# Second attention spread behind weight tiles, first attention with two pairs of score banks, in a kernel of two transformer blocks

## The reference, cut to what matters

```python
s = q @ k.T * scale (+ bias)
p = softmax(s)                  # differential: p1 - lam * p2, then an RMS norm of the output
o = p @ v
x = x + gt_a * (concat(o) @ w_out)
```

```python
q_a, k_a, v_a, q_b, k_b, v_b, f_logit, g_a, g_b = split(hn @ w_in)
a = causal_attention(q_a, k_a, v_a, bias=-slope * distance)     # 8 "moba" heads
b = causal_attention(q_b, k_b, v_b, bias=c_q - c_k)             # 8 "fox" heads, c = cumsum(log_sigmoid(f_logit))
merged = sigmoid(g_a) * (a @ w_proj_a) + sigmoid(g_b) * (b @ w_proj_b)
x = x + merged @ w_out
```

## Time and profile before

| | before |
|---|---|
| median of 3 runs | 2947.49 us |
| the profiled execution's own time | 2962.96 us |
| its span in the profile | 2961.1 us |
| TensorE, matmuls busy | 2801.1 us (95%) |
| VectorE busy | 1785.9 us (60%) |
| ScalarE busy | 1155.6 us (39%) |
| mean granted TensorE clock | 0.977 of full |
| first attention | from 479.6 to 639.6 us, with three of its four output units |
| second attention | from 1780.3 us, its own steps alone until the first gate unit at 1853.7 us |

### The profile page before, as it was taken

How to read it: one execution, slowest core, us unless ns; L and a number is a source line. 1 busy time by engine, 2 the same in 40 slices (tenths; PEclk the granted TensorE clock), 3 DMA queues, 4 the chain that set the end, 5 groups by cost and what they waited for, 6 DMA issues and landing times.

```text
span 2961.1 us, 33601 instructions
## 1 busy us (share of the span) xinstructions
PE 2801.1 (95%) x12559; PEld 2248.7 (76%) x12559; DVE 1785.9 (60%) x1973; ACT 1155.6 (39%) x1485; POOL 393.8 (13%) x298
## 2 busy tenths in 40 slices
PE   5999999898999999999989998999999999999997
PEld 1587786577777888888767886888787888888885
DVE  2479964766699555555564447455455566566565
ACT  3132233434333444444343434444443444444443
POOL 2124304101777000000060000000000000000000
PEclk9999998999999999999999999999999999999998
DMA  9988962235776655555445560555555655556552
GB/s 353 313 289 302 320 227 86 71 143 196 260 240 225 216 195 184 191 192 194 159 171 180 189 198 29 185 194 190 169 181 180 194 184 188 195 184 188 194 184 99
DMA packets 286271, 579.88 MB, mean 196 GB/s; under 512 B 14034, under 2 KB 18546, under 8 KB 283886
## 3 DMA queue, kind: packets, MB, share of 16 engines
q1 hardware_dynamic: 277176, 542.55, 55.3%
q0 software_dynamic: 7152, 35.33, 3.3%
q10 hardware_dynamic: 1862, 0.92, 0.1%
HBM read 573.63 MB, written 5.14 MB: 195 GB/s over the span
## 4 chain that ended last, share of the span: by engine, by line
issue 59%; PE 25%; POOLq 6%; DVE 4%; DMA 3%; POOL 2%; ACT 1%; DVEq 1%; SPq 0%; ACTq 0%
PE bank L361 6%; PE bank L363 6%; PE bank L362 6%; POOLq L2074 2%; PE bank L619 2%; POOLq L2076 2%; DMA w_raw<-in_w_ada 1%; POOLq L2083 1%; DVE proj_ctx L1449 1%; POOLq L2081 1%; DMA b_rows<-in_b_ada 1%; PE bank L1755 1%; PE bank L655 1%; ACT probs L729 1%; DVE w_lo L357 1%
## 5 line engine op out<-in xcount | busy, mean ns | idle before, releaser
L357 DVE TENSOR_TENSOR w_lo<-w_raw,w_hi 128x1024 fp32r<-128x1024 f32 (+2 forms) x856 | 1139.5, 1354 | 636.4 <-ACT w_hi L349 624.4
L349 ACT ACTIVATE w_hi<-w_raw 128x1024 fp32r<-128x1024 f32 (+2 forms) x856 | 894.3, 1056 | 1313.1 <-PE bank L363 1150.5
L361 PE MATMUL bank<-w_hi,xa_hi 128*128 128x512 f32 (+1 forms) x2304 | 907.4, 394 | 27.4 <-DVE w_lo L357 22.8
L363 PE MATMUL bank<-w_hi,xa_lo 128*128 128x512 f32 (+1 forms) x2304 | 898.3, 390 | 0.0
L362 PE MATMUL bank<-w_lo,xa_hi 128*128 128x512 f32 (+1 forms) x2304 | 898.3, 390 | 0.0
L361 PEld LDWEIGHTS bank<-w_hi,xa_hi 128*128 128x128 f32 x2304 | 435.2, 189 | 131.2 <-DVE w_lo L357 19.7
L363 PEld LDWEIGHTS bank<-w_hi,xa_lo 128*128 128x128 f32 x2304 | 435.0, 189 | 90.4
L362 PEld LDWEIGHTS bank<-w_lo,xa_hi 128*128 128x128 f32 x2304 | 435.4, 189 | 88.1 <-issue 0.7
L361 PE MATMUL bank<-w_hi,ffn_act_hi 128*128 128x512 f32 x864 | 339.5, 393 | 12.9 <-DVE w_lo L357 12.9
L362 PE MATMUL bank<-w_lo,ffn_act_hi 128*128 128x512 f32 x864 | 338.1, 391 | 0.0
L363 PE MATMUL bank<-w_hi,ffn_act_lo 128*128 128x512 f32 x864 | 337.9, 391 | 0.0
(11 more groups left out here) (274 smaller groups left out, 1896.7 us busy)
## 6 DMA issues: line engine op xcount, KB each, us to landing
w_raw<-in_w_in SPq DMA_DIRECT2D x116, 1024.0 KB, 5.1
w_raw<-in_w_ada SPq DMA_DIRECT2D x80, 1024.0 KB, 6.6
w_raw<-in_w_up SPq DMA_DIRECT2D x64, 1024.0 KB, 5.3
w_raw<-in_w_down SPq DMA_DIRECT2D x64, 1024.0 KB, 5.2
w_raw<-in_ffn_wg SPq DMA_DIRECT2D x44, 1024.0 KB, 5.2
w_raw<-in_ffn_wu SPq DMA_DIRECT2D x44, 1024.0 KB, 5.2
w_raw<-in_ffn_wd SPq DMA_DIRECT2D x44, 1024.0 KB, 5.1
w_raw<-in_w_out SPq DMA_DIRECT2D x32, 1024.0 KB, 5.1
```

Of the source, the lines that this page charges most:

```text
L349: act.activation(whi[:, slot, ks, 0:w], raw[:, q, ks, 0:w], ACT.Copy)\
L357: dve.tensor_tensor(wlo[:, slot, ks, 0:w], raw[:, q, ks, 0:w], whi[:, slot, ks, 0:w].bitcast(F32), ALU.subtract).then_inc(sem("lo_made"), 1)
L361: pe.matmul(out, xh, wh, start=first, stop=False)
L363: return pe.matmul(out, xl, wh, start=False, stop=last)
```

## The change

The class `Attn` and its three functions go; each attention gets its own functions of one step.

**Second attention.** Units of the column blocks 6 to 11 and of the first gate block (28 units, v = 0 to 27) are written out, and behind 19 of them stands one step of the attention: behind v = 1, 3, ... 15 the steps n = 0 to 7, behind v = 17 to 27 the steps n = 8 to 18. Scores use one bank, turned probabilities one, turned keys and queries one, outputs one. The cumulated forget sum of all fox heads is made once (n = 1) and added by one float32 matmul for each half of the scores.

**First attention.** Scores get two pairs of banks, turned probabilities a single bank used twice in a step (first copied out by ScalarE, then by VectorE), outputs one bank. Probabilities are turned at n-3, values made at n-4. Step 0's keys and queries are turned ahead of the last unit, (9, 3). `hi` and `lo` of the first two output units move into steps 3 and 5.

```diff
+HOOK_BEHIND = {2 * n + 1: n for n in range(8)} | {9 + n: n for n in range(8, N_HEADS2 + 3)}
+        OUT_SPLIT = {3: 0, 5: 1, len(STEPS) + 1: 2, len(STEPS) + 2: 3}
+        def s_bank(n, i):
+            return ps[2 + 2 * (n % 2) + i]
+        def att1_pe(pe, n):
+            s = valued(n - 6)
+            if s and s["kind"] == "diff":
+                pe.wait_ge(sem("diff_normed"), s["head"] + 1)
...
+            if s and s["turn"]:
+                wait(pe, "att_qk_copied", s["a"])
...
+            s = valued(n - 3)
+            if s:
+                pe.wait_ge(sem("att_probs"), n - 2)
+                wait(pe, "att_pt_copied_d", s["d"])
+                att1_turn_probs(pe, n - 3, 0)
+            s = step(n - 1)
+            if s:
+                pe.wait_ge(sem("att_qk_copied"), s["a"] + 1)
+                wait(pe, "att_exp_done", n - 2)
...
+            s = valued(n - 3)
+            if s:
+                pe.wait_ge(sem("att_pt_copied_a"), s["d"] + 1)
+                att1_turn_probs(pe, n - 3, 1)
+            s = valued(n - 4)
...
+        def att1_act(act, n):
...
+        def att1_dve(dve, n):
...
+        def att2_pe(pe, n):
+            if 0 <= n - 1 < N_HEADS2:
+                s, r = STEPS2[n - 1], (n - 1) % 2
+                pe.wait_ge(sem("att2_qk_copied"), n)
+                wait(pe, "att2_negmax", n - 1)
...
+                for i in range(2):
+                    bank = ps[5][:, i * SEQ:(i + 1) * SEQ]
+                    m = pe.matmul(bank, qT2[:, r, i * P:i * P + P], kT2[:, r, :], start=True, stop=not fox)
+                    if fox:
+                        m = pe.matmul(bank, ident[:, s["head"]:s["head"] + 1].to_broadcast([P, P]), decay[:, :],
+                                      start=False, stop=True)
+            if n < N_HEADS2:
+                wait(pe, "att2_qk_copied", n)
...
+            d = n - 2
+            if 0 <= d < N_HEADS2:
+                pe.wait_ge(sem("att2_probs"), d + 1)
+                wait(pe, "att2_pt_copied", d)
...
+            if n == 1:
+                for j in range(2):
+                    m = pe.matmul(ps[7][0:8, 0:SEQ], nlf[:, j, :], tri[:, j, :], start=j == 0, stop=j == 1)
+            d = n - 3
+            if 0 <= d < N_HEADS2:
+                pe.wait_ge(sem("att2_pt_copied"), d + 1)
+                wait(pe, "att2_out_lo", d)
...
@@ ScalarE
-            hi(act, U_OUT // 4, 0)
             behind(len(W) - 2)
-            hi(act, U_OUT // 4, 1)
+            act.wait_ge(sem("rotated_pe"), 1)
+            att1_act(act, 0)
             behind(len(W) - 1)
...
+            for n in range(1, H1 + 6):
+                att1_act(act, n)
+                if n in OUT_SPLIT:
+                    hi(act, U_OUT // 4, OUT_SPLIT[n])
...
+            for v in range(29):
+                u = U_WIN2 + 24 + v
+                hi(act, u // 4, u % 4)
+                if v % 4 == 1 and v < 28:
+                    c = 5 + v // 4
+                    qkv2_copy(c, c % 2)
+                if v - 1 in HOOK_BEHIND:
+                    att2_act(act, HOOK_BEHIND[v - 1])
@@ VectorE: the same with lo, att1_dve and att2_dve
@@ TensorE
+                if (c, k) == (9, 2):
+                    pe.wait_ge(sem("mla_copied_a"), 3)
+                    pe.wait_ge(sem("mla_copied_d"), 3)
+                    pe.wait_ge(sem("rotated_pe"), 1)
+                    att1_pe(pe, 0)
+            for n in range(1, H1 + 6):
+                att1_pe(pe, n)
+                if n - H1 in (0, 1, 2):
...
+                    unit(pe, U_OUT // 4, q, ps[0:2], XA, 4 * BY_HEADS[q], q == 0, False)
...
+            for v in range(28):
...
+                unit(pe, U_WIN2 // 4 + c, q, ps[2 * b:2 * b + 2], XA, 4 * q, q == 0, q == 3)
+                if v in HOOK_BEHIND:
+                    att2_pe(pe, HOOK_BEHIND[v])
@@ GpSimd
+            pool.wait_ge(sem("x2_stored"), 16)
+            pool.memset(decay[:, :], 0.0)
```

More of the change, by code:

```diff
@@ L827, in build, with step, valued, last_of_turn @@
-        A1 = Attn("att", STEPS, 4, kT, qT, probs, probsT, XA)
-        A2 = Attn("att2", STEPS2, 2, kT2, qT2, probs2, probsT2, XB)
+        H1 = len(STEPS)
+        def step(n):
+            return STEPS[n] if 0 <= n < H1 else None
+        def valued(n):
+            s = step(n)
+            return s if s and s["d"] is not None else None
+        def last_of_turn(a):
+            return max(i for i, s in enumerate(STEPS) if s["a"] == a)
+        def values_to(n):
+            return sum(1 for s in STEPS[:max(n, 0)] if s["d"] is not None)
@@ new lines, in att2_act @@
+        def att2_act(act, n):
+            if n == 0:
+                act.wait_ge(sem("x2_stored"), 16)
+            if n < N_HEADS2:
+                act.wait_ge(sem("att2_qk_turned"), n + 1)
+                wait(act, "att2_scores", n - 1)
+                act.activation(kT2[:, n % 2, :], ps[4][:, 0:SEQ], ACT.Copy)
+                act.activation(qT2[:, n % 2, :], ps[4][:, SEQ:2 * SEQ], ACT.Copy).then_inc(sem("att2_qk_copied"), 1)
+            if n == 1:
+                act.wait_ge(sem("f_acc"), 2)
+                act.wait_ge(sem("decay_zeroed"), 1)
+                act.activation(decay[0:8, :], ps[7][0:8, 0:SEQ], ACT.Copy).then_inc(sem("fz_act"), 1)
+            d = n - 3
+            if 0 <= d < N_HEADS2:
+                act.wait_ge(sem("att2_out"), d + 1)
+                act.activation(XB[0][:, srcs_of(STEPS2[d])["o"], :], ps[7][:, 0:SEQ], ACT.Copy)\
+                    .then_inc(sem("att2_out_hi"), 1)
+            if 0 <= n - 1 < N_HEADS2:
+                par = (n - 1) % 2
+                act.wait_ge(sem("att2_negmax"), n)
+                for i in range(2):
+                    m = act.activation(probs2[:, par, i, :], probs2[:, par, i, :], ACT.Exp, bias=stat(NM + 2 * par + i),
+                                       scale=HD ** -0.5, accum_out=stat(SUM + 2 * par + i))
+                m.then_inc(sem("att2_exp_done"), 1)
@@ L1348, in _ @@
             qkv2(0, True)
-            with act.Fori(1, N_QKV2 // 2) as i:
+            with act.Fori(1, 3) as i:
                 qkv2(i)
-            qkv2_copy(N_QKV2 - 1, 1)
             act.wait_ge(sem("fz_dve"), 1)
@@ L1374, in merge @@
                     hi(act, g, q)
-                hi(act, g + 1, 0)
+                if not first:
+                    hi(act, g + 1, 0)
                 hi(act, g + 1, 1)
@@ L1660, in _ @@
             dve.tensor_scalar(nlf[:, :, :], fz[:, 4], float(HD) ** 0.5, None, ALU.mult).then_inc(sem("nlf_made"), 1)
-            lo(dve, U_MRG // 4, 0)
-            lo(dve, U_MRG // 4, 1)
-            dve.wait_ge(sem("masks_loaded"), 48)
-            dve.wait_ge(sem("x2_stored"), 16)
-            attn_dve(dve, A2, 0, len(STEPS2), U_MRG)
+            for v in range(29):
+                u = U_WIN2 + 24 + v
+                lo(dve, u // 4, u % 4)
+                if v % 4 == 1 and v < 28:
+                    c = 5 + v // 4
+                    qkv2_copy(c, c % 2)
+                if v - 1 in HOOK_BEHIND:
+                    att2_dve(dve, HOOK_BEHIND[v - 1])
             def gate_mul(n):
@@ L1686, in merge @@
                     lo(dve, g, 3)
-                for q in range(4):
+                for q in range(int(first), 4):
                     lo(dve, g + 1, q)
```

506 lines of the change are left out of this document (246 added, 260 removed).

## The result

The changed kernel takes **2913.97 us** (median of 4 runs, 2912.36 to 2917.41) against 2948.22 of the kernel before beside it (4 runs, 2946.53 to 2956.4): ratio 0.988, 95% interval 0.986 to 0.990, 34.3 us less. I had forecast 2916.3 in a range of 2903 to 2931.

A forecast was written before the change was run, and what follows sets the result against it. Weight stretches were taken as bound by TensorE; in the attentions it waits, in the first for a VectorE and ScalarE chain. Gains of 25.3 (second attention) and 5.9 (first), 31.2 off the 2947.49 median, gave 2916.3 us, range 2903 to 2931.

The forecast's parts named there:

- Rival 3: Second attention: steps wait because normalisation comes later than TensorE asks; 0.5 us at 11 steps, 2922 us; chance 0.13.
- (a): First attention's start: TensorE newly waits for the rotations behind unit (9, 2), 2.9 us, between 2.8 and 3.6.
- (b): First attention's start: the turning of step 0 itself takes 0.9 us.
- (c): First attention's start: the gap lowers the clock, 2.5 us lost.
- rival 2: The new waits cost nothing of the clock and g_row lands in time: gain 39.5 us, 2908 us; chance 0.2.
- rival 1: First attention: half clock lasts through MLA, 10.5 us less gain, 20.7 left, 2926.8 us; chance 0.17.
- (d): First attention, from the end of (9, 3) through MLA and a moved output unit to step 4's exponential: 31.4 us.
- (e): First attention: the second moved output unit hits the chain, 3.5 us.
- (f): First attention, steps 5 to 12: eight links take 42.3 us, before 43.9.
- rival 4: First attention isn't decoupled at all: it gives nothing net or loses 5 us, 2922 to 2927 us; chance 0.12.
- (g): First attention, on to step 19, grouped-query and neighbourhood steps: 43.9 us, a neighbourhood step 6.15.
- (h): First attention, behind the last exponential: 20.8 us with three units in it, so 4.5 us.

The follow-up runs named there:

- e1: Changed kernel with only the second attention as changed, the first as in the kernel before: 2921.9 us, ratio 0.9913 to the kernel before.
- e6: Changed kernel, but each fox step adds its decay by triangle products, two float32 matmuls for each half, as before: 2923.7 us, ratio 0.9917.
- e4: Changed kernel, but hi and lo of the first two output units stand ahead of the first attention again: 2917.2 us, ratio 0.9901.
- e2: Kernel before with only the first attention as changed, the second as it was: 2943.0 us, ratio 0.999.
- e7: Changed kernel; in neighbourhood rounds scores precede the first turn of probabilities, and ScalarE copies turned probabilities ahead of the next k and q: 2918.1 us.
- e11: Changed kernel, g_row loaded first; in the last three rounds scores first, ScalarE copying turned probabilities, then the output, then k and q: 2914.5 us.
- e8: Changed kernel, but g_row is loaded ahead of x_one, both behind the last values instead of the last lo: 2911.4 us, ratio 0.9878.
- e3: Changed kernel, but step 0 of the first attention is turned behind the last unit (9, 3) again: 2917.0 us, ratio 0.9901.
- e5: Changed kernel with step 0 turned behind (9, 3) and hi and lo of the first two output units ahead of the first attention: 2923.1 us.
- e9: Changed kernel with one pair of score banks, so scores wait for the exponential of the step before: 2936.8 us, ratio 0.9964.

## Why the prediction was right

**Second attention** (forecast 25.3, measured 25.1 like for like and 26.6 with the spell of before; e1 alone 25.4 by medians). Step by step: a fox step 3.50 us, forecast 3.46 and 0.05 for borders; the decay 0.87 for each (e6: 6.96 us for eight, forecast 7.0); no waits (0.2 us in 520). Rival 3 is refused by what the probabilities had in hand, 2.0 us and with a copy in between 1.3, forecast 1.5 and 0.7. What is left of 75.6 us is 50.5, forecast 50.3.

**First attention**, in the terms of the prediction, all from one timeline of the changed kernel (end of (9, 3) 479.56; reciprocal of step 4 at 513.73, of 12 at 556.71, of 19 at 602.36):

- (a), (b), (c): forecast 2.9 + 0.9 + 2.5; measured 1.77 + 0.93 + 0. The wait was mis-sized because I let one operation shrink where two did. The Trainium skill (SBUF — State Buffer, Who interferes with whom) says that a VectorE instruction with two inputs in SBUF contends with a GpSimd instruction that reads SBUF; the trace agrees, 1.44 and 1.25 us in e4 against 0.46 us. The half clock did not come: rival 2 was right on this term and rival 1 wrong, and e4 shows none behind 3.55 us either.
- (d) forecast 31.4 to the exponential of step 4, measured 30.9 (510.48); three times 4.2 + 0.9 is 15.3, where I had written 15.6. (e) forecast 3.5; the reciprocal came 3.25 us later. But e4 says that both moved units cost at most 2.7 us, not 7.0: without them something else holds the chain for most of that time. The milestones agree because they are read with the units in place; the price of one edit was not the length of its operation.
- (f) forecast 42.3, measured 43.0, and 41.6 in e2, which has less half clock there: "differential pairs of 11.2 us" came out at 9.9 and 10.7 us between exponentials (the first, of 13.4, holds the second moved unit), and one of 12.2 at the end of a spell of half clock (534 to 546), 10.8 in e2. A pair under 10 us was one of my own signs of being wrong: the links with a sum or a norm are 0.3 to 0.7 us shorter than I added up. The old kernel took 43.9 for the same links, so the eight steps together gained 0.9 to 2.3 us only. There rival 4 was near the truth; about the attention as a whole it was wrong.
- (g) forecast 43.9, measured 45.6. The step that failed is "neighbourhood 6.15" (1.4 + 4.66 is 6.06, a slip besides): the four links take 27.8 us where I had 24.6, and the rest of (g), 1.5 us shorter than forecast, hid half of it. I followed VectorE's chain and left out that the mask overwrites probabilities that TensorE turns through one bank, half by half (e7, e11: 6.96 us with it, mostly 6.0 without).
- (h) forecast 4.5, measured 23.07 less three units, 6.75: the copies between two turnings are bare (0.69 us of idle, twice) and the last lo costs 0.93 us.

Sum 132.3 for 131.9: the errors, -4.4 us in (a) to (e) and +4.7 in (f) to (h), cancelled. **Given back behind it**: forecast 5.8, measured 3.4, with the wait of VectorE for g_row (3.73 us) and TensorE's gap in the place named (2.81 us for 4.4). The gap grew by 1.7 us, not 3.3, and the half clock behind it (644 to 648) cost some 1.6, not 2.5; e8 shows cause and price. So the first attention's net is 8.0 by the two traces, 3.7 to 9.5 by the other profiled runs with the same code, and 4.3 to 8.0 by medians, where I said 5.9. The total, 31.2 for 34.3, is well inside what such spells move.

What I did not see at all is why the start ran at half clock before: I spoke of the gap and not of its maker. e3 and e5 show it, ScalarE's queue. Half clock avoided is most of the first attention's gain: 9.7 of 11.3 us are TensorE's own records at a higher clock, and undoing the two edits at the start loses 6.0 (e5). And my sentence that the new order "gives back what the free scores gain" was right in direction, with larger amounts: e9 prices the free scores at 19.4 us, 7.3 of them waits and 12.2 clock, and what else is new costs 8.1 us against the old; that it is the order alone isn't shown.

## What to carry to other kernels

Where an attention is a chain over two engines and weight units wait behind it, put the steps between the units and count, for the tightest interval, when each hand-over is ready and when it is asked for; here 1.3 to 2 us in hand were enough for 25 us of gain. A move that looks like a small cover (one turn a unit earlier) can be worth its effect on another engine's queue and on the clock: ask what stands ahead of the copy, not only ahead of the product. Don't move an operation behind the maximum, a mask or any long neighbour without looking who holds the bank it frees: the links became shorter and one head lost it all.

## What was not expected of the hardware

The length of a gap didn't say how long the clock stayed low behind it: 14 us in e5, 24 in e1 and 27 in the kernel before behind 4.26 us, 4 us in e3 behind 2.34 and 14 in e9 behind 2.23, with TensorE busy nearly throughout, and none in e4 behind 3.55 us, where the dense weights of (9, 3) followed. And the same instructions did not always meet the same clock. Between 515 and 530 us there was no spell in e2, 4 us in the changed kernel and 14 us in e8, which cost e8 4.7 us in two links, with the same instructions up to there. What decides this the runs don't tell; no run varied it by itself. It is as large as several of the terms that I added up, and a reason to read a stretch in more than one kernel.
